# Two fused transformer blocks on one core: one-stage routing with a split router, the output matrix by row halves, linear heads normed beside the product

## The chip, the cores and the metric

One NeuronCore of a Trainium2 chip runs the whole program. The metric is the device time of one execution in microseconds (us), the median of several runs. The engines are PE (TensorE, matmuls), DVE (VectorE), ACT (ScalarE), POOL (GpSimd) and SP (SyncE, which issues the transfers). Tensors are fp32; the big products are made in three fp32r passes of a high and a low part.

## The reference

256 tokens of width 1024 pass a first block (attention, spatial gating, cross attention, 16 routed experts) and a second of two layers. What the change touches:

```python
def hierarchical_moe(h, w_rg, b_rg, w_re, b_re, w_gate, w_up, w_down):   # block 1, h = rms_norm(x, g_moe)
    glog = (t @ w_rg + b_rg); gprob = softmax(glog); gval, gidx = top_k(gprob, 1)
    elog = (t @ w_re + b_re).reshape(-1, N_GROUPS, EXPERTS_PER_GROUP)
    evals, eidx = top_k(elog of group gidx, TOP_K); ew = softmax(evals) * gval
    for e in range(N_EXPERTS): y += combine[:, e:e+1] * ((silu(t @ w_gate[e]) * (t @ w_up[e])) @ w_down[e])

for i in range(DEPTH_2):                                                 # block 2
    u = rms_norm_2(h, norm_attn[i]) @ w_in[i]
    o_a = nsa_attention(...)                                             # mix columns 0..255
    o_b = diff_attention(...)       # rms_norm_2(o, sub_gain) * (1 - lam_init)     256..511
    o_c = gla_mixer(...)            # rms_norm_2(o, norm_gain) * silu(og)          512..767
    o_d = hgrn2_mixer(...)          # rms_norm_2(o, norm_gain) * silu(og)          768..1023
    h = h + concatenate([o_a, o_b, o_c, o_d]) @ w_out[i]
    c = rms_norm_2(h, norm_ffn[i])
    h = h + (swiglu(c) if i % 2 == 0 else moe_swiglu(c, router, ...))    # layer 1: top 2 of 8 experts
    h = h + (p[i] @ ple_w_proj[i]) * sigmoid(rms_norm_2(h, ple_norm[i]) @ ple_w_gate[i])
```

## The kernel before, in words

All weights stream through a ring of 12 raw pieces of 512 KB. SP loads them in the fixed order in which `stream_matrix` and `Experts` add them; ACT makes the high part of a piece (`make_hi`, line 403), DVE the low part (`make_lo`, line 408), both into rings of four; PE multiplies three times (lines 424 to 426) and counts the piece as used. The next two pieces of a product are split ahead, as "early" ones.

The program is a sequence of stages. In a stage every engine runs its own instructions, ordered by semaphores; a stage ends when all engines are through. Each stage is written out by hand, and nothing reorders it.

The first routing is `clear_routing` (the gain row's load, zeroing), `normed_T` (ACT squares and root, line 528 on; DVE scales x; then the stage of `transposes`, lines 480, 518, 502), `route` (the router in full fp32, line 1585, the logits turned, then about thirty tiny DVE steps that pick experts, lines 1618 to 1644 and 2980 to 2993), `place_tokens` (PE counts, DVE writes positions, the dispatch table `disp`, line 2552, and the return table `ret`, line 2555) and `first_gather` (PE gathers tokens for the first four experts bank by bank, line 1286, and DVE and ACT copy banks in turn, line 1297). The second one, in layer 1, is alike without the stacked tables.

The mixers of a layer (`hybrid_mixers`) project, attend (`attend`), add the two halves of each differential head (line 2139), prepare gates, and run the linear pipeline for GLA and HGRN2: PE makes exponents (2316 to 2318) and products (2350), ACT exponentials (2392), DVE decays (2430) and masks (2441), and ACT writes heads into `mix` (2396). Behind it stand `group_norms` for three kinds of heads, a stage that multiplies with the gates (2480), `transposes` of all of `mix` (line 480), and `product` with `w_out`, column chunk by column chunk, each over all rows of the matrix, which adds into x (line 624). Beside this product p is turned.

## Time and profile before

| what | us |
|---|---|
| median of 3 runs (lowest, highest) | 2504.54 (2499.8, 2505.14) |
| the profiled execution, device time | 2508.09 |
| its span in the profile | 2506.3 |
| PE busy | 2270.1 (91%) |
| DVE busy | 1867.1 (74%) |
| ACT busy | 1528.3 (61%) |
| POOL busy | 50.5 (2%) |

Busy shares are averages over stages of very different kind: the two routed expert stages and the dense one fill most of the span, and the routings and mixers are short stages between them. For a change in a short stage one reads that stage's timeline: which engine works, and which waits for it.

### The profile page before, as it was taken

The page shows a single profiled execution, that of the slowest core. Times are in us where ns is not written, and L with a number is a line of the kernel's source. Part 1 is how long each engine was busy: PE and PEld are TensorE (multiplying, and loading weights), DVE is VectorE, ACT ScalarE, POOL GpSimd, SP SyncE. Part 2 cuts the span into 40 slices and gives each one's busy share as a digit, 9 for nine tenths or more (in the row PEclk, how much of TensorE's full clock was granted, in tenths as well). Part 3 has the DMA queues.
Part 4 walks back from the last instruction along what each step waited for, and adds up shares of the span by engine and source line. Part 5 has one row for each costly group of instructions (what it writes and reads, how often), then busy time and mean ns, then how long its engine had stood idle before and what let it go on. Part 6 is the DMA issues. An engine that isn't in the chain of part 4 may idle for free. (4 is left out here: it accounts for less than half of the span.)

```text
span 2506.3 us, 36936 instructions
## 1 busy us (share of the span) xinstructions
PE 2270.1 (91%) x11988; PEld 1858.2 (74%) x11988; DVE 1867.1 (74%) x2075; ACT 1528.3 (61%) x1997; POOL 50.5 (2%) x61
## 2 busy tenths in 40 slices
PE   7988589998987699988986689999999999999997
PEld 6777467776765599976765478888888888888885
DVE  4655588886755645545766569999999999999995
ACT  4554288886532344435532358787878787878784
POOL 0000000000001100000003000000000000000000
PEclk9989799999987899998987789999999999999998
DMA  8433099996630066644620079999999999999991
GB/s 297 134 128 107 9 373 361 353 342 239 188 101 1 22 219 185 186 148 143 179 67 2 30 251 376 336 372 336 377 334 371 336 375 335 374 335 374 336 375 67
DMA packets 280552, 593.81 MB, mean 237 GB/s; under 512 B 26208, under 2 KB 39424, under 8 KB 280320
## 3 DMA queue, kind: packets, MB, share of 16 engines
q1 hardware_dynamic: 280448, 592.45, 66.6%
q8 instruction: 62, 1.02, 0.2%
q14 instruction: 42, 0.34, 0.0%
HBM read 591.32 MB, written 1.05 MB: 236 GB/s over the span
## 5 line engine op out<-in xcount | busy, mean ns | idle before, releaser
L408 DVE TENSOR_TENSOR ring_lo<-ring,ring_hi 128x1024 fp32r<-128x1024 f32 (+1 forms) x1120 | 1337.9, 1215 | 306.8 <-ACT ring_hi L403 249.7
L403 ACT ACTIVATE ring_hi<-ring 128x1024 fp32r<-128x1024 f32 (+1 forms) x1120 | 1162.2, 1053 | 486.0 <-PE psum L426 432.7
L424 PE MATMUL psum<-ring_hi,xg_hi 128*128 128x512 f32 x896 | 356.2, 398 | 5.9 <-PEq L189 3.5
L426 PE MATMUL psum<-ring_hi,xg_lo 128*128 128x512 f32 x896 | 351.0, 392 | 0.0
L425 PE MATMUL psum<-ring_lo,xg_hi 128*128 128x512 f32 x896 | 350.3, 391 | 0.0
L424 PE MATMUL psum<-ring_hi,xT_hi 128*128 128x512 f32 (+2 forms) x512 | 201.5, 394 | 19.2 <-DVE ring_lo L408 10.3
L424 PEld LDWEIGHTS psum<-ring_hi,xg_hi 128*128 128x128 f32 x896 | 169.4, 189 | 40.0 <-issue 3.7
L426 PE MATMUL psum<-ring_hi,xT_lo 128*128 128x512 f32 (+2 forms) x512 | 197.8, 386 | 0.0
L425 PE MATMUL psum<-ring_lo,xT_hi 128*128 128x512 f32 (+2 forms) x512 | 197.7, 386 | 0.0
L426 PEld LDWEIGHTS psum<-ring_hi,xg_lo 128*128 128x128 f32 x896 | 169.1, 189 | 36.3
L425 PEld LDWEIGHTS psum<-ring_lo,xg_hi 128*128 128x128 f32 x896 | 169.6, 189 | 33.9
L424 PE MATMUL psum<-ring_hi,hT_hi 128*128 128x512 f32 x448 | 176.3, 394 | 8.8 <-DVE x L1210 5.2
L425 PE MATMUL psum<-ring_lo,hT_hi 128*128 128x512 f32 x448 | 175.1, 391 | 0.0
L426 PE MATMUL psum<-ring_hi,hT_lo 128*128 128x512 f32 x448 | 175.1, 391 | 0.0
L424 PE MATMUL psum<-xT_hi,ring_hi 128*128 128x256 f32 x480 | 137.2, 286 | 3.2 <-PEq L189 3.2
L425 PE MATMUL psum<-xT_lo,ring_hi 128*128 128x256 f32 x480 | 137.0, 285 | 0.0
L426 PE MATMUL psum<-xT_hi,ring_lo 128*128 128x256 f32 x480 | 136.9, 285 | 0.0
L424 PEld LDWEIGHTS psum<-ring_hi,xT_hi 128*128 128x128 f32 x512 | 98.8, 193 | 40.7 <-DVE ring_lo L408 9.4
L1327 PE MATMUL psum<-ring_hi,xg 128*128 128x512 f32 x256 | 108.8, 425 | 5.8 <-DVE ring_lo L408 3.8
L426 PEld LDWEIGHTS psum<-ring_hi,xT_lo 128*128 128x128 f32 x512 | 98.6, 192 | 19.6
L425 PEld LDWEIGHTS psum<-ring_lo,xT_hi 128*128 128x128 f32 x512 | 99.1, 194 | 18.3
L424 PEld LDWEIGHTS psum<-ring_hi,hT_hi 128*128 128x128 f32 x448 | 84.6, 189 | 29.5 <-issue 12.4
(501 smaller groups left out, 3242.8 us busy)
## 6 DMA issues: line engine op xcount, KB each, us to landing
ring<-in_moe_w_gate_dram SPq DMA_DIRECT2D x224, 512.0 KB, 5.3
ring<-in_moe_w_up_dram SPq DMA_DIRECT2D x224, 512.0 KB, 5.5
ring<-in_moe_w_down_dram SPq DMA_DIRECT2D x224, 512.0 KB, 4.9
ring<-in_w_in_dram SPq DMA_DIRECT2D x76, 512.0 KB, 5.1
ring<-in_w_gate_dram SPq DMA_DIRECT2D x64, 512.0 KB, 5.0
ring<-in_w_up_dram SPq DMA_DIRECT2D x64, 512.0 KB, 5.6
ring<-in_w_down_dram SPq DMA_DIRECT2D x64, 512.0 KB, 5.4
ring<-in_ffn_w_gate_dram SPq DMA_DIRECT2D x28, 512.0 KB, 3.7
```

The lines of the kernel that those rows point to most:

```text
L403: sc.activation(raw_view(ring_hi, FINE, num, a, width), raw_view(ring, RAW, num, a, width), ACT.Copy) \
L408: v.tensor_tensor(raw_view(ring_lo, FINE, num, a, width), raw_view(ring, RAW, num, a, width), raw_view(ring_hi, FINE, num, a, width).bitca ...
L424: pe.matmul(out_, lhsT[0], rhs[0], start=start, stop=False)
L425: pe.matmul(out_, lhsT[0], rhs[1], start=False, stop=False)
L426: return pe.matmul(out_, lhsT[1], rhs[0], start=False, stop=stop)
L1327: pe.matmul(to, lhsT, w[0], start=start, stop=False)
```

## The change

It computes the same. Four things are done.

Routing in one stage. `route` turns x as it is, while ACT squares it; the gain is multiplied into the router's columns, the logits are scaled by 1/rms afterwards. Router and x are split into high and low parts, and 32 fp32r matmuls take the place of 16 in full fp32. Tokens are scaled by one DVE instruction per half. The low parts of the tokens are made in `place_tokens`, the return table in `first_gather`, where ACT makes all copies. As the turned tokens are no longer normed, the branch that runs all tokens through all experts (not taken with these inputs) turns them itself.

Output matrix by row halves. `w_out` streams its upper four row pieces for both column chunks, then the lower ones.

Softmax heads early. The NSA and differential heads (the upper rows' inputs) are normed and turned at the start of the linear pipeline's stage. The add of the differential pairs is a step of `attend`.

Linear heads beside the product. Its first four pieces need only the softmax heads; meanwhile ACT and DVE norm and gate the linear ones, whose norm gain is a column now, applied when the turned heads are copied. Several tiles (`sq_wide`, `kv_twice`, `qkT`) lie in parts of `mix` and `u` that are free at the time.

```diff
+    def stream_matrix_by_halves(w):
+        for half in range(2):
+            for c in range(0, D, FF):
+                for q in range(2 * half, 2 * half + 2):
+                    ws.add(w[q * 2 * P:(q + 1) * 2 * P, c:c + FF].rearrange("(a p) n -> p a n", p=P), 2, FF)
...
+                        if "pairs_to" in j:
+                            both = j["dst"].rearrange("p (n c) d -> p n c d", c=2)
+                            step(v.tensor_tensor(j["pairs_to"], both[:, :, 0, :], both[:, :, 1, :], ALU.add))
...
-                        for k in range(0, KT, 2):
-                            e.wait_ge(g.sem, g.at(k + 1))
-                            l.inc(copy_gathered(v.tensor_copy, k, 0, bank(k)))
...
+                        for half in range(HALVES):
+                            for c in range(2):
+                                l.inc(v.tensor_tensor(ret[:, half, :, c * SLOTS:(c + 1) * SLOTS], disp[:, half, :, :].bitcast(F32),
+                                                      last_bc(comb[:, half, 1:E + 1], SLOTS), ALU.mult))
...
-                        for k in range(1, KT, 2):
+                        for k in range(KT):
...
+    def routed_experts(xn, stacked=None, meanwhile=lambda step: None, placed=lambda: None):
+        place_tokens(N_EXP2 if routed[0] else N_EXP1, stacked, meanwhile)
+        placed()
...
+    def route(gain, row, w, n, xn, finish):
         done, summed, copied = S("router_ready"), S("router_summed"), S("router_copied")
+        turned_x, x_hi, x_lo, w_scaled, w_hi, w_lo = (S(n) for n in ("transposed", "hi_ready", "lo_copied", "squares_scaled", "gates_ready",
+                                                                     "gates_plus_one"))
+        sq, act, rms_done, dve = S("squares_summed"), S("act_chain"), S("rms_done"), S("dve_chain")
...
+                    for b in range(4):
+                        for m in range(4):
+                            k, h = 2 * b + m // 2, m % 2
+                            last = pe.transpose(bank(where[b])[:, m * P:(m + 1) * P], x[:, h, k * P:(k + 1) * P], ident)
+                        turned_x.inc(last)
+                    e.wait_ge(w_lo.sem, w_lo.at(1))
                     for k in range(KT):
-                        for m, part in enumerate(xT):
-                            last = pe.matmul(bank(2)[0:n, 0:SEQ], w[:, k, :], part[:, k, :].bitcast(F32),
-                                             start=(k == 0 and m == 0), stop=(k == KT - 1 and m == 1))
+                        if k % 2 == 0:
+                            e.wait_ge(x_lo.sem, x_lo.at(k // 2 + 1))
+                        for i, w_ in enumerate(w_split):
+                            for j, x_ in enumerate(xT):
+                                last = pe.matmul(bank(2)[0:n, 0:SEQ], w_[:, k, :], x_[:, k, :], start=(k == 0 and i == 0 and j == 0),
+                                                 stop=(k == KT - 1 and i == 1 and j == 1))
...
+                def scalar_first(e):
+                    e.wait_ge(w_scaled.sem, w_scaled.at(1))
+                    w_hi.inc(sc.copy(w_split[0][:], w[:]))
+                    for b in range(4):
+                        e.wait_ge(turned_x.sem, turned_x.at(b + 1))
+                        x_hi.inc(sc.copy(pair_of(xT[0], b), bank(where[b])))
+                    use_table(LOG_EXP)
+                    for h in range(HALVES):
+                        sq.inc(sc.activation(junk[:, h, :], x[:, h, :], ACT.Square, accum_out=ss[:, h:h + 1]))
+                    e.wait_ge(sq.sem, sq.at(HALVES))
+                    act.inc(sc.activation(rms[:], ss[:], ACT.Ln, scale=1.0 / D, bias=eps))
+                    e.wait_ge(act.sem, act.total)
+                    rms_done.inc(sc.activation(rinv[:], rms[:], ACT.Exp, scale=-0.5))
...
+                def vector_first(e, ready):
+                    w_scaled.inc(v.tensor_tensor(w[:], w[:], last_bc(gain[:], n), ALU.mult))
+                    for t in (comb, chosen, place):
+                        dve.inc(v.memset(t[:], 0.0))
+                    dve.inc(v.memset(bank(3, 2), 0.0))
+                    e.wait_ge(w_hi.sem, w_hi.at(1))
+                    w_lo.inc(v.tensor_tensor(w_split[1][:], w[:], w_split[0][:].bitcast(F32), ALU.subtract))
+                    for b in range(4):
+                        e.wait_ge(x_hi.sem, x_hi.at(b + 1))
+                        x_lo.inc(v.tensor_tensor(pair_of(xT[1], b), bank(where[b]), pair_of(xT[0], b).bitcast(F32), ALU.subtract))
+                    e.wait_ge(rms_done.sem, rms_done.at(1))
+                    e.wait_ge(gain_loaded.sem, gain_loaded.total)
+                    for h in range(HALVES):
+                        ready.inc(v.scalar_tensor_tensor(out=xn[:, h, :], in0=x[:, h, :], scalar=rinv[:, h:h + 1], in1=gain_row[:],
+                                                         op0=ALU.mult, op1=ALU.mult))
+                    e.wait_ge(done.sem, done.at(1))
...
-        gla_gain = par("gla_gain", [P, HD], A["gla_norm_2"][layer].partition_broadcast(P))
-        hg_gain = par("hgrn_gain", [P, HD], A["hgrn_norm_2"][layer].partition_broadcast(P))
+        gain_cols = tmp(L2, "linear_gains", [P, 2])
+        for n, name in enumerate(("gla_norm_2", "hgrn_norm_2")):
+            for half in range(2):
+                loads.append((gain_cols[half * HD:(half + 1) * HD, n:n + 1], A[name][layer].rearrange("(d one) -> d one", one=1)))
...
+                          pairs_to=od[:, h, n0 // 2:n0 // 2 + 2, :],
...
+                        else:
+                            e.wait_ge(y_lo.sem, y_lo.at(m + 1))
...
+                    for b in range(2):
+                        if b:
+                            e.wait_ge(od_normed.sem, od_normed.at(1))
+                        for m in range(4):
+                            k, h = 2 * b + m // 2, m % 2
+                            last = pe.transpose(bank(6 + b)[:, m * P:(m + 1) * P], mix[:, h, k * P:(k + 1) * P], ident)
+                        turned_y.inc(last)
...
+                    for b in range(2):
+                        e.wait_ge(turned_y.sem, turned_y.at(b + 1))
+                        y_hi.inc(sc.copy(pair_of(xT[0], b), bank(6 + b)))
...
+                    step(v.tensor_scalar(d_norm[:], d_norm[:], 1.0 - lam_init, None, ALU.mult))
+                    e.wait_ge(od_squared.sem, od_squared.at(1))
+                    step(v.tensor_reduce(od_ss, od_sq, AXX, ALU.add), od_summed)
+                    e.wait_ge(od_root.sem, od_root.at(1))
+                    step(v.tensor_tensor(od, od, last_bc(od_rt, HD), ALU.mult))
+                    step(v.tensor_tensor(od, od, row_bc(d_norm[:], [HALVES, MH]), ALU.mult), od_normed)
...
+                    for b in range(2):
+                        e.wait_ge(y_hi.sem, y_hi.at(b + 1))
+                        y_lo.inc(v.tensor_tensor(pair_of(xT[1], b), bank(6 + b), pair_of(xT[0], b).bitcast(F32), ALU.subtract))
...
+            order = [(c, 2 * half + q) for half in range(2) for c in range(2) for q in range(2)]
...
+                    for i, (p, (c, q)) in enumerate(zip(got, order)):
+                        if i == 4:
+                            e.wait_ge(y_lo.sem, y_lo.at(2))
+                        e.wait_ge(lo_ready, p.n + 1)
+                        w = [raw_view(r, FINE, (p.n, 0), 2, FF) for r in (ring_hi, ring_lo)]
+                        for a in range(2):
+                            k = 2 * q + a
+                            for h in range(HALVES):
+                                last = three_passes(bank(2 * c + h), [x_[:, k, h * P:(h + 1) * P] for x_ in xT],
+                                                    [w_[:, a, :] for w_ in w], k == 0, k == KT - 1)
+                        last.then_inc(used, 1)
+                        if i == 2:
+                            for b in range(2):
+                                e.wait_ge(normed.sem, normed.at(b + 1))
+                                for m in range(4):
+                                    k, h = 4 + 2 * b + m // 2, m % 2
+                                    last = pe.transpose(bank(4 + b)[:, m * P:(m + 1) * P], mix[:, h, k * P:(k + 1) * P], ident)
+                                turned_y.inc(last)
...
+                    squared.inc(sc.activation(squares[:], both, ACT.Square))
+                    make_his(e, not_early(got[:4]))
+                    e.wait_ge(sums.sem, sums.at(1))
+                    act.inc(sc.activation(rt[:], ss[:], ACT.Ln, scale=1.0 / HD, bias=eps))
+                    e.wait_ge(act.sem, act.total)
+                    roots.inc(sc.activation(rt[:], rt[:], ACT.Exp, scale=-0.5))
+                    use_table(SILU)
+                    for n in ("gog", "rog"):
+                        gates.inc(sc.activation(uc(n), uc(n), ACT.Silu))
+                    for b in range(2):
+                        e.wait_ge(turned_y.sem, turned_y.at(b + 1))
+                        y_hi.inc(sc.activation(pair_of(xT[0], 2 + b), bank(4 + b), ACT.Copy, scale=gain_cols[:, b:b + 1]))
+                    make_his(e, got[4:])
+                    use_table(LOG_EXP)
+                    e.wait_ge(p_turned.sem, p_turned.at(1))
+                    p_hi.inc(sc.copy(flat(pT)[0], bank(6)))
+                    make_his(e, early)
+                @block.vector
+                def _(e):
+                    e.wait_ge(squared.sem, squared.at(1))
+                    sums.inc(v.tensor_reduce(ss[:], squares[:], AXX, ALU.add))
+                    make_los(e, not_early(got[:4]))
+                    e.wait_ge(roots.sem, roots.at(1))
+                    dve.inc(v.tensor_tensor(both, both, last_bc(rt[:], HD), ALU.mult))
+                    e.wait_ge(dve.sem, dve.total)
+                    for b, n in enumerate(("gog", "rog")):
+                        at = slice(512 + b * 256, 768 + b * 256)
+                        e.wait_ge(gates.sem, gates.at(b + 1))
+                        normed.inc(v.tensor_tensor(mix[:, :, at], mix[:, :, at], uc(n), ALU.mult))
+                    for b in range(2):
+                        e.wait_ge(y_hi.sem, y_hi.at(b + 1))
+                        y_lo.inc(v.scalar_tensor_tensor(out=pair_of(xT[1], 2 + b), in0=bank(4 + b), scalar=gain_cols[:, b:b + 1],
+                                                        in1=pair_of(xT[0], 2 + b).bitcast(F32), op0=ALU.mult, op1=ALU.subtract))
+                    make_los(e, got[4:])
...
-                            for c in range(2):
-                                dve.inc(v.tensor_tensor(ret[:, h, :, c * SLOTS:(c + 1) * SLOTS], disp[:, h, :, :].bitcast(F32),
-                                                        last_bc(comb[:, h, 1:n + 1], SLOTS), ALU.mult))
...
+    def low_tokens(step):
+        step(v.tensor_tensor(xn_split[1][:], xn[:], xn_split[0][:].bitcast(F32), ALU.subtract))
+    routed_experts(xn_split, (disp1, ret1), low_tokens, routing.close)
```

How the instructions stand. First DVE from the last product's stage to the first pick of the first routing, before (a branch closes or opens a stage; `xn_rows` are the tokens, `gl` and `el` the logits):

```order
L554 TENSOR_SCALAR xn_rows<-x,rinv 128x1024 x2
L189 UNCONDITIONAL_BRANCH
L491 UNCONDITIONAL_BRANCH
L502 SCALAR_TENSOR_TENSOR xT_lo<-psum,c_g_moe,xT_hi 128x256 x8
L189 UNCONDITIONAL_BRANCH
L2973 UNCONDITIONAL_BRANCH
L1604 TENSOR_TENSOR xn_rows<-xn_rows,gain_row 128x2048
L2978 TENSOR_TENSOR xn_moe_lo<-xn_rows,xn_moe_hi 128x2048
L2980 TENSOR_TENSOR gl<-psum,r_b_rg 128x8
L2981 TENSOR_TENSOR el<-psum,r_b_re 128x32
L1618 TENSOR_REDUCE gbest<-gl 128x2
```

and in the changed kernel the same place, in one stage:

```order
L1686 TENSOR_TENSOR router_lo<-router,router_hi 128x160
L1689 TENSOR_TENSOR xT_lo<-psum,xT_hi 128x512 x4
L1693 SCALAR_TENSOR_TENSOR xn_rows<-x,rinv,gain_row 128x1024 x2
L3162 SCALAR_TENSOR_TENSOR gl<-psum,rinv,r_b_rg 128x4
L3164 SCALAR_TENSOR_TENSOR el<-psum,rinv,r_b_re 128x16
L3162 SCALAR_TENSOR_TENSOR gl<-psum,rinv,r_b_rg 128x4
L3164 SCALAR_TENSOR_TENSOR el<-psum,rinv,r_b_re 128x16
L1713 TENSOR_REDUCE gbest<-gl 128x2
```

Three changes of stage are gone, and a scaling that had waited for a stage of its own stands ahead of the logits, which now need the root.

Then DVE behind the linear pipeline, before: the norms, the gates, the turned heads' low parts and the output product with its pieces (`ring_lo`), four stages.

```order
L701 UNCONDITIONAL_BRANCH
L704 TENSOR_TENSOR sq<-mix 128x512 x3
L707 TENSOR_REDUCE gss<-sq 128x8 x3
L710 TENSOR_TENSOR mix<-mix,grt 128x2x256
L712 TENSOR_TENSOR mix<-mix,diff_norm 128x2x256
L710 TENSOR_TENSOR mix<-mix,grt 128x2x256
L712 TENSOR_TENSOR mix<-mix,gla_gain 128x2x256
L710 TENSOR_TENSOR mix<-mix,grt 128x2x256
L712 TENSOR_TENSOR mix<-mix,hgrn_gain 128x2x256
L189 UNCONDITIONAL_BRANCH
L2477 UNCONDITIONAL_BRANCH
L2480 TENSOR_TENSOR mix<-mix,u_111 128x2x256 x2
```

In the changed kernel the linear heads' work stands between low parts of the product's own pieces (`out_sums`, `out_roots` and `linear_gains` belong to them):

```order
L2661 UNCONDITIONAL_BRANCH
L2664 TENSOR_REDUCE out_sums<-out_squares 128x16
L416 TENSOR_TENSOR ring_lo<-ring,ring_hi 128x1024 x2
L2667 TENSOR_TENSOR mix<-mix,out_roots 128x2x512
L2672 TENSOR_TENSOR mix<-mix,u_116 128x2x256 x2
L2675 SCALAR_TENSOR_TENSOR xT_lo<-psum,linear_gains,xT_hi 128x512 x2
L416 TENSOR_TENSOR ring_lo<-ring,ring_hi 128x1024 x4
L2687 TENSOR_TENSOR x<-x,psum 128x512 x2
```

The heads' scaling now stands behind two pieces' low parts and ahead of four others.

Last PE at the opening of the linear pipeline (`lg` and `u` hold the logs of the gates, QD and KD the decayed queries and keys), before:

```order
L2316 MATMUL psum<-consts,lg 128x512
L2317 MATMUL psum<-consts,lg 128x384
L2318 MATMUL psum<-consts,lg 128x128
L2350 MATMUL psum<-QD,KD 64x64 x24
L2350 MATMUL psum<-qkT 64x64 x4
L2352 MATMUL psum<-QD,KD 128x64 x2
```

and in the changed kernel:

```order
L2418 MATMUL psum<-consts,lg 128x512
L2419 MATMUL psum<-consts,lg 128x384
L2420 MATMUL psum<-consts,lg 128x128
L2481 MATMUL psum<-consts,mix 128x128 x8
L2452 MATMUL psum<-QD,KD 64x64 x24
L2452 MATMUL psum<-u_116 64x64 x4
L2454 MATMUL psum<-QD,KD 128x64 x2
```

Eight transposes of `mix` have come between the second unit's exponents and the first products.

## Rows read from the trace of the kernel before

**Rows 1.** Windows over two stretches of the expert stages (busy us, instructions):

```profile
380.00:580.00 200.00, 200.00 (x909) 145.37 (x908) 174.19 (x180) 167.00 (x224) 0.00 (x0) 1.00 0.96 351
...
1500.00:2400.00 900.00, 894.90 (x4154) 742.94 (x4153) 834.68 (x769) 705.13 (x733) 0.00 (x0) 1.00 0.97 355
```

**Rows 2.** Timeline of DVE, first routing (start, duration, line, operands, idle before):

```profile
266.17 1.29 DVE L624 TENSOR_TENSOR x<-x,psum 128x512 f32<-128x512 f32 x2 [1.88 <-PE psum L426]
...
283.95 2.29 DVE L2978 TENSOR_TENSOR xn_moe_lo<-xn_rows,xn_moe_hi 128x2048 fp32r<-128x2048 f32 x1 [2.04 <-ACT xn_moe_hi L3000]
...
289.66 0.16 DVE L1618 TENSOR_REDUCE gbest<-gl 128x2 f32<-128x8 f32 x1
...
296.43 0.19 DVE L2993 TENSOR_TENSOR chosen<-m,goh 128x32 f32<-128x32 f32 x1
...
305.34 2.36 DVE L2555 TENSOR_TENSOR return_p<-dispatch,comb 128x1024 f32<-128x1024 f32 x2
```

**Rows 3.** Timeline of ACT in the same stretch:

```profile
269.40 1.06 ACT L528 ACTIVATE xn_rows<-x 128x1024 f32<-128x1024 f32 x1 [7.55 <-PEq L189]
...
271.94 0.20 ACT L533 ACTIVATE rinv<-rms 128x2 f32<-128x2 f32 x1
...
313.62 0.59 ACT L1297 CAST xg<-psum 128x512 fp32r<-128x512 f32 x1 [0.37 <-PE psum L1286]
```

**Rows 4.** Timeline of PE, the gather of the first routing:

```profile
312.23 0.40 PE L1286 MATMUL psum<-dispatch,xn_moe_lo 128*128 128x256 f32 x2
312.47 0.40 PE L1286 MATMUL psum<-dispatch,xn_moe_hi 128*128 128x256 f32 x2
```

**Rows 5.** Windows before the first routing, and where the linear pipeline ends:

```profile
253.30:256.80 3.50, 3.43 (x8) 2.78 (x9) 2.31 (x2) 2.00 (x2) 0.00 (x0) 0.52 0.02 5
256.80:266.00 9.20, 9.20 (x41) 7.32 (x39) 3.61 (x5) 2.12 (x2) 0.00 (x0) 1.00 0.00 0
266.00:268.00 2.00, 0.13 (x1) 0.00 (x0) 1.47 (x5) 0.00 (x0) 0.00 (x0) 1.00 0.00 0
824.00:830.00 6.00, 2.63 (x12) 2.30 (x12) 1.50 (x3) 0.99 (x4) 2.18 (x5) 0.74 0.00 0
```

**Rows 6.** Timelines of ACT, PE and DVE, tail of layer 0's mixers:

```profile
828.93 0.27 ACT L2396 COPY mix<-psum 128x128 f32<-128x128 f32 x1 [3.30 <-PE psum L2367]
...
839.55 3.65 PE L480 MATMUL psum<-consts,mix 128*128 128x128 f32 x16 [10.65 <-PEq L189]
...
844.87 0.47 PE L424 MATMUL psum<-ring_hi,xT_hi 128*128 128x512 f32 x1 [1.68 <-PEq L189]
...
867.43 0.69 DVE L624 TENSOR_TENSOR x<-x,psum 128x512 f32<-128x512 f32 x1 [3.06 <-PE psum L426]
```

**Rows 7.** Timeline of DVE, second routing:

```profile
1414.42 1.29 DVE L624 TENSOR_TENSOR x<-x,psum 128x512 f32<-128x512 f32 x2 [3.06 <-PE psum L426]
...
1437.56 0.17 DVE L1618 TENSOR_REDUCE best<-lg 128x2 f32<-128x16 f32 x1
...
1441.58 0.17 DVE L1644 TENSOR_TENSOR comb<-one,one 128x16 f32<-128x16 f32 x1
```

**Rows 8.** Timeline of ACT, the tail's table load:

```profile
833.90 1.28 ACT L201 ACT_TABLE_LOAD   x1
```

**Rows 9.** The page's costliest groups, splitting of weights:

```profile
L408 DVE TENSOR_TENSOR ring_lo<-ring,ring_hi 128x1024 fp32r<-128x1024 f32 (+1 forms) x1120 | 1337.9, 1215 | 306.8 <-ACT ring_hi L403 249.7
L403 ACT ACTIVATE ring_hi<-ring 128x1024 fp32r<-128x1024 f32 (+1 forms) x1120 | 1162.2, 1053 | 486.0 <-PE psum L426 432.7
```

**Rows 10.** Timeline of DVE, start of the linear pipeline:

```profile
794.02 1.23 DVE L2441 TENSOR_TENSOR pairs<-psum,consts 128x1024 f32<-128x1024 f32 x1 [3.06 <-PE psum L2352]
```

**Rows 11.** Timeline of DVE, the pairs stage:

```profile
774.77 0.76 DVE L2139 TENSOR_TENSOR mix<-o 128x256 f32<-128x256 f32 x2 [0.54 <-PEq L189]
```

**Rows 12.** Timelines of DVE and SP, start of layer 0:

```profile
631.48 2.36 DVE L2018 TENSOR_TENSOR mix<-x,g_final 128x1024 f32<-128x1024 f32 x2 [6.72 <-DMA g_final<-in_g_final_dram]
...
620.07 0.43 SPq L460 DMA_DIRECT2D hgrn_gain<-in_hgrn_norm_dram  x1
```

More of the change, by code:

```diff
@@ L1576, in route, with _ @@
         with ExitStack() as st:
             logits_T = tmp(st, "logits_T", [n, SEQ])
+            gain_row = tmp(st, "gain_row", [P, D])
+            junk = tmp(st, "x_squares", [P, HALVES, D])
+            ss, rms, rinv = (tmp(st, name, [P, HALVES]) for name in ("ss", "rms", "rinv"))
+            w_split = tmp_split(st, "router", [P, KT, n])
             with stage() as block:
-                sync_stage(block)
+                @block.sync
+                def _(sp):
+                    gain_loaded.inc(sp.dma_start(gain_row[:], row.partition_broadcast(P)), 16)
+                    issue_loads(sp)
@@ L2502, in build, with place_tokens @@
     largest = ctx.enter_context(nc.sbuf_tensor("largest_count", [P, 1], mybir.dt.int32))
-    def clear_routing(gain_row, src):
-        with stage() as block:
-            @block.sync
-            def _(sp):
-                gain_loaded.inc(sp.dma_start(gain_row[:], src.partition_broadcast(P)), 16)
-                issue_loads(sp)
-            dve = S("dve_chain")
-            @block.vector
-            def _(e):
-                for t in (comb, chosen, place):
-                    last = v.memset(t[:], 0.0)
-                v.memset(bank(3, 2), 0.0)
-                dve.inc(last)
-    def place_tokens(n, stacked):
+    def place_tokens(n, stacked, meanwhile):
         counted, dve = S("tokens_counted"), S("dve_chain")
@@ L3017, in build @@
         pT = tmp_split(ple, "pT", [P, PLE // P, SEQ])
[L3018 to L3039 removed]
+        with ExitStack() as L2:
+            hybrid_mixers(layer, L2, pr, pT)
         moe_x = ExitStack()
         xn = tmp(moe_x, "xn_moe", [P, HALVES, D])
[L3043 to L3046 removed]
         if layer % 2 == 0:
+            normed_T(x, g_ffn2[layer], xT, xn)
             all_tokens_experts(lambda h, ex: const("all_ones")[:, 0:1])
```

276 lines of the change are left out of this document (150 added, 126 removed).

## The prediction, as it was recorded before the result

> **What bounds the kernel now.** I read the windows over the long stretches first. In the first routed experts and in the second the matmul engine is busy for 200.00 of 200 us and 894.90 of 900, at full clock, while the DMA share is 0.96 and 0.97 [rows 1]. Nothing in those stages is edited, so they cost what they cost; what can move is the time ahead of them. The ring of weights is full when they begin, in both kernels with the same pieces, so a stage that ends earlier moves all behind it by the same amount.
>
> So I read the timelines of the short stages next. In them engines take turns. In the first routing the products' last add ends at 267.46 (266.17 + 1.29), the first pick of a maximum stands at 289.66, the last mask at 296.43, and the last of the return tables is written at 307.70 (305.34 + 2.36) [rows 2]. In the mixers' tail ScalarE writes the last linear head at 829.20, TensorE turns `mix` at 839.55, starts the product at 844.87, and VectorE gets the result at 867.43 [rows 6]. The long idle times in brackets there (10.65 before the transposes) say that TensorE waits for stages in which only VectorE and ScalarE work.
>
> **First routing, one stage for four.** Before, 22.2 us lie between 267.46 and 289.66. New, on ScalarE: about 0.7 for the router's high part, four copies of a bank at 0.59 that follow each other at some 0.55 (2.3), then two squares and the root, which took 2.7 before, from 269.40 to 272.14 [rows 3]: rinv at 5.7 after the stage opens. Then VectorE scales x by rinv and the gain row, two instructions of 1024 columns. No such form is in the trace; the nearest row takes 2.29 for 2048 columns of two tensors [rows 2], so 2.3 for both, 8.0. The gain row's transfer is issued at the stage's start and has these 5.7 us. Four small ops on the logits (0.16 to 0.2 each) give 8.7. TensorE is beside it: 16 transposes, then 32 matmuls of 256 columns in place of 16 in full fp32. Matmuls of the new kind and width start 0.24 apart for two (312.23 to 312.47) [rows 4]. 32 x 0.12 = 3.9 from 2.5 on is 6.4, with copy and turning back 7.3: hidden below the 8.0 of VectorE. At half clock the matmuls take 7.7, end at 10.2, and the picks start at 11.4 instead of 8.7. The clock is at 1.00 in the 2 us after the product [rows 5], the transposes now fall into these, so I take mostly full clock. With 0.35 for the stage change the saving is 22.2 - 9.05 = 13.1 at full and 10.4 at half clock; I take **12.0**. The high part of the tokens (one copy of 2048 columns, two times 1.0) now lies beside the last picks, which have 2.1 us left after the exponential; uncovered it would cost 2. The low part (2.29) lies beside the counting matmuls, which VectorE waited for.
>
> **Place and gather.** The return tables leave VectorE's chain: 2 x 2.36 = **4.7** saved [rows 2]. They go to the gather stage, beside TensorE, where VectorE has no copies any more; ScalarE takes all eight, 0.59 each [rows 3]. A bank is four matmuls, so one comes every 0.48 at full and 0.96 at half clock; in a mixture of both the eighth copy ends some 0.3 later than the one that stood at 313.62 (0 to 1.2): **+0.3**.
>
> **Second routing.** Add ends at 1415.71, first pick at 1437.56, end at 1441.75 [rows 7]: 21.85 before, 8.9 or 11.5 new: 12.9 or 10.3, taken as **12.0**. Its placing is not changed.
>
> **The tails, twice.** Before, 38.2 us from 829.20 to 867.43; the product alone is 22.5 of it [rows 6]. New: 0.35 stage change, 22.5 product, 8 transposes in the middle (16 took 3.65 at half clock [rows 6], so 0.9 for 8 at full), and a start at half clock. That start is a row that speaks against the change. The old 16 transposes ran just ahead of the product, and the product then started fast. Where a product starts after idling, 8 matmuls take 3.43 us at 0.52 of the clock, against 41 in 9.20 at 1.00 [rows 5], 1.6 lost; the end of the linear pipeline stands at 0.74 [rows 5]. I take 2.2 (0 to 2.7).
>
> Does the new chain beside it stay hidden? ScalarE: squares 1.05, two high parts 2.0, root 0.5, table 1.28 [rows 8], two SiLU of 512 columns at 0.59 like the copies of that size [rows 3], 1.2: 6.0. VectorE: sums 1.2 (half of the 2.29 for 2048 columns), two low parts, then one scaling of 1024 columns and two gatings of 512, about 7.4. A high part costs 1.053 and a low part 1.215 by the page's groups [rows 9]. TensorE comes to its transposes after three pieces of 2.8, at 8.4 at the earliest and 9.9 with the slow start, so the cover is 1 to 2.5 us. Next late is the fifth piece: its high part can only follow the two copies of turned heads, low part ready near 14, TensorE there at 13.7: 0.3. Sum: 0.35 + 22.5 + 0.9 + 2.2 + 0.3 = 26.3, saving **11.9 per layer**, 23.8 (9.0 to 13.5 each).
>
> **What the linear pipeline pays.** Eight transposes stand between the second exponents and the first products; VectorE there waited 3.06 for TensorE [rows 10], so it is the path: 0.9 at full, 1.8 at half clock. The two low copies of VectorE wait for ScalarE's high ones and stand ahead of its first masking, and end about then. I take 1.5 (0.9 to 2.5), **+3.0** for two layers. The squares, sums and scalings of the differential heads lie in the first 4 us, in which VectorE waits for the first exponential; uncovered they would cost 2.5.
>
> **Small stages.** The stage that adds pairs (0.76, 0.54 idle ahead of it, about 775.9 at the next one's start [rows 11]) becomes one add of 128 columns behind the last output: **1.0 per layer** saved, 2.0.
>
> **Transfers.** Two broadcasts go, four columns of 64 words come: two more issues, 0.43 each on SP and a little between [rows 12], ahead of g_final, for which VectorE waits 6.72 until 631.48 [rows 12], with the second chunk's low parts queued behind it and TensorE behind those: **+0.95** in layer 0 (0 to 2). In layer 1 nobody waits for parameters so early.
>
> **Sum**: -12.0 - 4.7 + 0.3 - 12.0 - 23.8 + 3.0 - 2.0 + 0.95 = **-50.2 us**. The profiled execution took 2508.09 (span 2506.3 and 1.8 around it) and would take 2457.9. It is 3.6 above the median of the runs, 2504.54, from which I forecast **2454.3**. The ends of the terms together: 58 saved (13.1, 4.7, 12.9, 27, 2.4, less 1.8) gives 2446; 36 saved (10.4, 4.7 less 1.2, 10.3, 18, 1.4, less 5 and 2) gives 2468.
>
> **Rivals.** (a) The product keeps the half clock. Its transposes and waits break it up; 96 matmuls at 0.43 instead of 0.23 cost 19.5 per layer, 17.3 more than taken, so 2454.3 + 34.6 = 2489. Against it: after 3.43 us at 0.52 the product ahead of the first routing ran at 1.00 to its end [rows 5]. The Trainium skill, TensorE: Matmul & The Clock Gate, section HAM oscillation, warns of this: waits between groups of matmuls can drop the array to half rate each time. (b) The experts give the gain back: with DMA at 0.96 [rows 1], a start that is earlier for TensorE might meet transfers that are not. Then all ahead of the two routed stages but the 11.4 of layer 0's mixers is lost: 2493. Against it: transfers start with the stage, not by the clock on the wall. (c) The other side: the untaken branch of both expert stages grows by the code for turning tokens. If steps of the taken one got longer through instruction loading, 16 and 56 steps share it: 50.2 / 72 = 0.70 us a step is where it decides, and 1 us gives 2526. Against it: TensorE has no gap in 200 us of such steps [rows 1]. (d) The stages are merged but waits stay: heads turned late in the tails and half clock in both routers, 20 to 36 saved, 2468 to 2484.
>
> **Chances.** Forecast 0.76 (2446 to 2468), better than all ends 0.05, (d) 0.10, (a) 0.03, (b) 0.02, (c) 0.02, and 0.02 for anything that ends within 0.2% (5 us), which is about what a measurement tells from no change. Nearly all cases are faster: 0.96, same 0.02, slower 0.02. For 8 in 10 the range takes the forecast's and a little of its neighbours': 2444 to 2471.
>
> **What would show it.** Right: 8 to 10 us from the last add to the first pick in both routings; 26 us from the last linear head to the product's end; TensorE idle under 1 us inside that product; masking in the pipeline 1 to 2 us later after its stage opens; expert steps as long as before. Wrong: a granted clock near 0.5 through the product, TensorE waiting for `mix` or for the fifth piece's low part by more than 2 us, VectorE waiting for the gain row, or expert steps longer than before.

## The result and the profile after

The changed kernel took 2446.36 us, the median of 4 runs (2444.55 to 2454.46), where the kernel before took 2504.84 in the same session (4 runs, 2499.8 to 2507.61). The ratio is 0.977 with a 95% interval of 0.9751 to 0.9789: 58 us saved, where I had forecast 50.2. The profiled execution took 2447.15, its span is 2445.4. One later execution, of the run with the row of the final gain first, took 3279.52 us at a mean granted clock of 0.642, and its ratio leaves it out.

The page of the profile after begins so (the row PEclk is the granted clock in tenths over 40 slices):

```profile
span 2445.4 us, 36780 instructions
...
PE 2250.2 (92%) x11988; PEld 1849.2 (76%) x11988; DVE 1854.6 (76%) x2058; ACT 1529.0 (63%) x1995; POOL 50.4 (2%) x61
...
PEclk9989899999987899999977899999999999999998
```

First the experts, by windows of the kernel after (all engines, then PE's clock, DMA share, GB/s):

```profile
360.00:560.00 200.00, 200.00 (x909) 145.36 (x908) 174.24 (x179) 167.01 (x224) 0.00 (x0) 1.00 0.96 352
...
1440.00:2340.00 900.00, 894.89 (x4155) 742.89 (x4154) 835.12 (x768) 705.18 (x732) 0.00 (x0) 1.00 0.97 355
```

They answer to [rows 1] and are the same: 909 matmuls in 200 us as before. What was won ahead of these stages is kept behind them.

The first routing, in VectorE's timeline of the kernel after:

```profile
264.23 1.28 DVE L632 TENSOR_TENSOR x<-x,psum 128x512 f32<-128x512 f32 x2 [1.88 <-PE psum L434]
...
267.54 2.47 DVE L1689 TENSOR_TENSOR xT_lo<-psum,xT_hi 128x512 fp32r<-128x512 f32 x4
271.23 2.48 DVE L1693 SCALAR_TENSOR_TENSOR xn_rows<-x,rinv,gain_row 128x1024 f32<-128x1024 f32 x2 [1.21 <-ACT rinv L1676]
...
274.29 0.16 DVE L1713 TENSOR_REDUCE gbest<-gl 128x2 f32<-128x8 f32 x1
...
281.83 2.29 DVE L3195 TENSOR_TENSOR xn_moe_lo<-xn_rows,xn_moe_hi 128x2048 fp32r<-128x2048 f32 x1 [0.54 <-PEq L189]
...
285.29 2.49 DVE L2741 TENSOR_TENSOR dispatch<-consts,place 128x1024 fp32r<-128x1024 f32 x2
288.30 4.63 DVE L1328 TENSOR_TENSOR return_p<-dispatch,comb 128x1024 f32<-128x1024 f32 x4 [0.53 <-PEq L189]
```

From the last add's end (265.51) to the first pick are 8.78 us, where [rows 2] have 22.20. The return tables (4.63 for four) begin only when the dispatch tables are done and lie beside the gather. ScalarE and TensorE in that stage:

```profile
270.99 0.20 ACT L1676 ACTIVATE rinv<-rms 128x2 f32<-128x2 f32 x1
272.23 0.36 ACT L1678 COPY logits_T<-psum 20x256 f32<-20x256 f32 x1 [1.04 <-PE psum L1656]
```

```profile
268.37 0.28 PE L1656 MATMUL psum<-xT_hi,router_hi 128*20 128x256 f32 x1 [0.60 <-DVE xT_lo L1689]
...
271.92 0.28 PE L1656 MATMUL psum<-xT_lo,router_lo 128*20 128x256 f32 x1
```

The 32 split matmuls run from 268.37 to 272.2, and the granted clock is 1.00 from 266 to 275. VectorE's scaling of the tokens ends at 273.71, so TensorE is hidden, as supposed.

The tail of layer 0, timelines of ScalarE, TensorE and VectorE of the kernel after:

```profile
806.60 0.27 ACT L2507 COPY mix<-psum 128x128 f32<-128x128 f32 x1 [2.84 <-PE psum L2471]
```

```profile
807.17 0.76 PE L432 MATMUL psum<-ring_hi,xT_hi 128*128 128x512 f32 x1 [0.61 <-PEq L189]
...
811.10 0.40 PE L432 MATMUL psum<-ring_hi,xT_hi 128*128 128x512 f32 x1
...
817.24 1.03 PE L2632 MATMUL psum<-consts,mix 128*128 128x128 f32 x8
...
821.49 0.47 PE L432 MATMUL psum<-ring_hi,xT_hi 128*128 128x512 f32 x1 [0.49 <-DVE ring_lo L416]
```

```profile
812.90 1.29 DVE L2672 TENSOR_TENSOR mix<-mix,u 128x512 f32<-128x512 f32 x2
...
833.18 1.29 DVE L2687 TENSOR_TENSOR x<-x,psum 128x512 f32<-128x512 f32 x2 [1.54 <-PE psum L434]
```

The last head stands at 806.87 and the last add starts at 833.18: 26.31 us, where [rows 6] have 38.23. The transposes at 817.24 have no wait in brackets: the gated heads were done at 814.19. The product starts at half clock: 9 matmuls take the 3.93 us to 811.10, 0.44 each, and then they follow each other by 0.23. In the kernel before, the product started at full clock, and its first matmuls (844.87 on) are 0.23 apart.

Stage by stage, in us, from the two profiled executions:

| stretch | before | after | saved | forecast |
|---|---|---|---|---|
| routing 1, last add to first pick | 22.20 | 8.78 | 13.4 | 12.0 |
| first pick to the experts' first product | 25.90 | 21.82 | 4.1 | 4.4 |
| routing 2, last add to first pick | 21.85 | 8.50 | 13.35 | 12.0 |
| tail, layer 0 and layer 1 | 38.23, 38.23 | 26.31, 27.06 | 11.9, 11.2 | 11.9, 11.9 |
| linear pipeline to last head, both | 45.31, 40.86 | 45.00, 42.41 | 0.3, -1.55 | -1.5, -1.5 |
| last softmax output's start to the next stage, both | 2.15, 2.15 | 1.64, 1.30 | 0.5, 0.85 | 1.0, 1.0 |
| mixers' start to g_final, layer 0 | 14.58 | 14.10 | 0.5 | -0.95 |

The rows sum to 54.5. The spans differ by 60.9; the other 6 us lie in stretches where nothing was edited, 2.0 of them ahead of 266 us. The experiments had to say what these are.

### The profile page after: what moved, and what is told of

It is laid out like the page before. It is cut to its first block and busy times, and to the rows that moved or that the text cites. A ratio compares the mean times of both kernels' runs of the same rounds, so it can differ in the third digit from the quotient of the medians.

```text
span 2445.4 us, 36780 instructions
## 1 busy us (share of the span) xinstructions
PE 2250.2 (92%) x11988; PEld 1849.2 (76%) x11988; DVE 1854.6 (76%) x2058; ACT 1529.0 (63%) x1995; POOL 50.4 (2%) x61
## 5 line engine op out<-in xcount | busy, mean ns | idle before, releaser
L432 PE MATMUL psum<-ring_hi,xT_hi 128*128 128x512 f32 (+2 forms) x512 | 202.1, 395 | 17.9 <-DVE ring_lo L416 11.2
```

Of the source, the lines that this page charges most:

```text
L432: pe.matmul(out_, lhsT[0], rhs[0], start=start, stop=False)
```

## The experiments

Each is the changed kernel with one edit, unless said otherwise. All were timed against the kernel before on the same chip. The changed kernel itself ran beside its two parts and beside the run in which the product waits; the others are set against it by their ratios to the kernel before.

**The changed kernel again, and its two parts alone.** In the second only the functions of routing, placing and gather are changed, in the third only the mixers with their tail.

> The changed kernel itself, timed in more rounds beside the parts of the change, so that their savings can be added up against its own. The traces show 54.7 us saved in the edited stages (13.4 and 13.35 in the routings, 4.6 in placing, less 0.45 in the gather, 11.9 and 11.2 in the tails, 1.4 in the pairs stages, less 1.2 in the linear pipelines) and some 6 us in stretches where nothing was edited. If those 6 us are chance of one execution, the saving over many runs is nearer 55 (about 2450); if they belong to the change, it stays at 58 or more (2447 or less).

> Only the routing part: one stage for four, split router, return tables beside the gather; mixers as before. By the prediction's terms 12.0 + 4.7 - 0.3 + 12.0 = 28.4 saved; by the stages of the trace after 13.4 + 4.6 - 0.45 + 13.35 = 30.9. If the two parts of the change are independent, this saving and that of the mixers' part add up to the whole. Rival: the routing saves its 31 only where the mixers' part has moved other work, then clearly less than 28.

> Only the mixers' part: matrix by halves, heads turned in the linear pipeline, tail beside the product; routing as before. By the prediction's terms 23.8 - 3.0 + 2.0 - 0.95 = 21.85 saved; by the stages of the trace after 23.1 - 1.2 + 1.4 + 0.5 = 23.8. If the remainder of the whole saving (58.5 less 54.7) comes from the clock that the shorter mixers leave behind them, this one saves 26 to 28; if it is chance, 22 to 24.

Measured: the whole 2448.49 (ratio 0.9767, 0.9745 to 0.979); routing alone 2471.76 (0.9865, 0.9845 to 0.9886), 34 us saved; mixers alone 2476.47 (0.9882, 0.9863 to 0.9901), 30 us saved. Together 63 +- 7 beside 58 +- 6: they add up within what is measured, though each is above what was expected of it: 34 against 28.4 and 30.9, and 30 against 22 to 24 (chance) or 26 to 28 (the clock), so the mixers' run confirms neither. The whole saved 58 us again, against "nearer 55" if the rest were one execution's chance: the 4 us beyond the stages' sum are in the medians of both occasions.

The stages themselves repeat: 8.78 for the first routing in all three executions that have it, 26.31 again for the tail of layer 0, 26.41 with the mixers alone. What does not repeat is the unedited rest. From the tail of layer 0 to the stage ahead of layer 1's linear part are 455.12 us before, 452.69 and 452.70 in the two executions of the changed kernel, 451.13 with the routing alone, 453.34 with the mixers alone. (The pairs stage of layer 1 lies in this stretch and is 0.9 shorter where the mixers are edited; apart from it and the pair adds in `attend` the instructions are the same.) And the start of the program up to the first routing, edited nowhere, took from 261.9 to 269.4 us in the 14 profiled executions of this document.

One place shows where it comes from. Windows of TensorE (busy, count, granted clock, DMA share, GB/s) around the same wait of 3.8 us, of the kernel before and then of the one after:

```profile
1168.00:1171.00 3.00, 0.14 (x2) 1.00 0.03 11
1171.00:1174.00 3.00, 2.81 (x16) 0.60 0.24 70
1174.00:1177.00 3.00, 1.32 (x3) 0.50 0.28 57
1177.00:1180.00 3.00, 3.00 (x8) 0.50 0.52 142
1180.00:1183.00 3.00, 3.00 (x11) 0.69 0.78 264
```

```profile
1131.00:1134.00 3.00, 0.06 (x1) 1.00 0.31 109
1134.00:1137.00 3.00, 2.12 (x12) 0.72 0.14 40
1137.00:1140.00 3.00, 1.16 (x7) 0.71 0.43 68
1140.00:1143.00 3.00, 3.00 (x13) 1.00 0.33 57
```

Behind this idle time (1167.0 to 1170.9, and 1131.1 to 1134.9) the clock falls to 0.50 in both. Before it stays there to about 1181, some 10 us; after it is back at 1.00 by 1140. From the wait to the end of the next product this makes 2.5 of the 6 us. No instruction there was edited. In the other executions the stretch moves with no edit in it, so one pair of traces can't tell what of this belongs to the change.

**The product waits for all heads.**

```diff
-                        if i == 4:
+                        if i == 0:
+                            for b in range(2):
+                                e.wait_ge(normed.sem, normed.at(b + 1))
...
+                                turned_y.inc(last)
                             e.wait_ge(y_lo.sem, y_lo.at(2))
...
-                        if i == 2:
-                            for b in range(2):
...
```

> As the changed kernel, but the product of the output matrix starts only when all heads are turned and split, in the same one stage. Theory: the overlap is what the tail saves. The normed and gated linear heads stand 8.4 us after the stage opens, then 8 transposes (1 to 2), two high and two low parts (1.3 and 0.7 behind them): the product starts 11 to 12 us later than now, less the 1.3 to 1.9 that its interrupted middle costs: 9 to 10 us a layer dearer, 2465 or so. Rival: merging stages is what saves, the overlap little: less than 4 us a layer, under 2455.

Measured: 2469.38 (0.9845, 0.9819 to 0.987), 21 us above the changed kernel that ran beside it. The product now begins at 818.46, VectorE's last add at 843.53:

```profile
814.92 1.97 PE L2622 MATMUL psum<-consts,mix 128*128 128x128 f32 x8 [7.08 <-DVE mix L2671]
818.46 0.80 PE L432 MATMUL psum<-ring_hi,xT_hi 128*128 128x512 f32 x1 [1.56 <-DVE xT_lo L2674]
```

The tail takes 35.38 and 35.48 us. So of the 11.9 us of layer 0, the overlap gives 9.1, and all else together 2.85 (8.4 and 2.75 in layer 1). This rest is the merged stage and the softmax heads turned early, less the slow start of the product: here its first 12 matmuls run at half clock, to 823.74. The rival (merging is what saves) falls. The two tails make 17.5 of the 21 us; the other 3.5 lie outside them.

**The softmax heads turned in the tail** instead of the pipeline: their 8 transposes, high and low parts stand at the tail's start, with a wait on them ahead of the first piece.

> As the changed kernel, but the softmax heads are turned and split at the start of the tail instead of in the linear pipeline. The pipeline should get back what I charged it with, 1.5 us a layer: 40.9 long in layer 1 again instead of 42.4. The tail gets a chain of 8 transposes at half clock (1.9), a high part (0.6) and two low parts (1.3) ahead of the product, some 4 us. Net 2 to 3 us a layer dearer, 2453 to 2455. Rival: the transposes cost the pipeline nothing that lasts, then 4 us a layer dearer, 2457.

Measured: 2455.81 (0.9799, 0.978 to 0.9818), 0.3% above the changed kernel's ratio, 4 us by the stages of its trace. The tail grew to 29.37 and 29.82 (3.06 and 2.76 more, where I expected some 4). The pipelines took 42.17 and 43.86 where the changed kernel has 45.00 and 42.41: one 2.8 shorter, one 1.5 longer. So my 1.5 a layer can't be read from the whole length. Unedited, the pipeline of layer 0 took 45.31 and 43.41 in two executions, with the edit 43.06 to 45.13 in seven; the clock moves it more than the transposes do. It can be read at the first masking in layer 1, where the clock is alike: it starts 8.54 and 8.55 us after the pipeline without the transposes in it, 9.63 or 9.64 in six executions with them, and 8.65 here. They cost 1.1.

**The router unsplit**, 16 matmuls of hi and lo tokens by the whole matrix in full fp32.

```diff
-                        for i, w_ in enumerate(w_split):
-                            for j, x_ in enumerate(xT):
-                                last = pe.matmul(..., w_[:, k, :], x_[:, k, :], ...)
+                        for j, x_ in enumerate(xT):
+                            last = pe.matmul(..., w[:, k, :], x_[:, k, :].bitcast(F32), ...)
```

> As the changed kernel, but the router's matrix is not split: each of the 16 products of tokens and router runs in full fp32, in the same one stage (the router's split is still made and not used). In the trace after, the 32 short matmuls end at 272.2 and VectorE's scaling of the tokens at 273.6, so the matmuls are hidden by 0.4. Unsplit they took 8.7 us before at a changing clock, 6.9 at full: from 268.4 they end at 275.3, the picks start 2.5 to 3 us later in each routing, 5 to 6 us dearer in all (2453 or so). Rival: the split buys nothing since VectorE is the bound there, then 2448, no dearer.

Measured: 2456.35 (0.981, 0.9793 to 0.9827). VectorE of this run:

```profile
267.93 2.48 DVE L1692 SCALAR_TENSOR_TENSOR xn_rows<-x,rinv,gain_row 128x1024 f32<-128x1024 f32 x2 [1.20 <-ACT rinv L1675]
272.93 0.22 DVE L3161 SCALAR_TENSOR_TENSOR gl<-psum,rinv,r_b_rg 128x4 f32<-128x4 f32 x1 [2.52 <-PE psum L1660]
...
273.60 0.16 DVE L1712 TENSOR_REDUCE gbest<-gl 128x2 f32<-128x8 f32 x1
```

The wait of 2.52 us on TensorE stands where none was. From the last add to the picks are 11.39 us, 2.61 more, and 2.35 more in the second routing, 5.0 in both as expected; the ratios differ by more, 0.4% or 10 us, and the other 5 are not explained. The split is needed for the saving to be whole.

**The return tables back** among the dispatch tables, the gather's copies on VectorE and ScalarE in turn.

> As the changed kernel, but the return tables are written between the dispatch tables again, and the gather's copies go to VectorE and ScalarE in turn. The tables cost 2 x 2.36 on VectorE's chain; the copies in turn give back the 0.45 that ScalarE alone takes longer. 4.2 us dearer: dispatch to the experts' first product in the trace 7.9 instead of 3.2 us after the last table, about 2452. Rival: nothing, if the gather's end is set by TensorE and the clock: then no dearer than 1 us.

Measured: 2454.0 (0.9805, 0.978 to 0.9831). From the first pick to the experts' first product: 25.82 us instead of 21.82. The tables cost 4.0, net of the gather's copies: nearly the whole of 4.1. By the ratios this run is 9 us dearer; the other 5 are not explained.

**The row of the final gain first**, with a semaphore of its own.

```diff
+                        if with_final:
+                            gain_loaded.inc(sp.dma_start(g_row[:], ...), 16)
                         for dst, src in loads:
                             params_loaded.inc(sp.dma_start(dst, src), 16)
```

> As the changed kernel, but in the mixers' first stage of layer 0 the row of the final gain is fetched first and has a semaphore of its own, where before VectorE waited for all 14 small transfers, the last of them this one (issued 6.4 us after the first, landed 7.7 after its issue, waited for 6.25 us). If the place in the queue is what it waits for, it lands 6 us earlier, ScalarE's root (606.3) becomes the last, and TensorE's gap of 3.55 us before the second chunk closes: 3 to 5 us saved, 2444. Rival: the row waits for transfers of weights that were issued before all of them, lands hardly earlier, and nothing is saved.

Measured: 2446.19 (0.9767, 0.9752 to 0.9782), no difference in the median. The issues of this row, of the changed kernel and of this one (KB, us to landing):

```profile
g_final<-in_g_final_dram SPq DMA_DIRECT2D x1, 512.0 KB, 7.7
```

```profile
g_final<-in_g_final_dram SPq DMA_DIRECT2D x1, 512.0 KB, 5.6
```

The row is used 7.77 us after the stage's start instead of 14.10, and VectorE, which waited 6.25 us in the changed kernel (first row), no longer waits for it:

```profile
611.34 2.36 DVE L2118 TENSOR_TENSOR mix<-x,g_final 128x1024 f32<-128x1024 f32 x2 [6.25 <-DMA g_final<-in_g_final_dram]
```

```profile
605.17 2.36 DVE L416 TENSOR_TENSOR ring_lo<-ring,ring_hi 128x1024 fp32r<-128x1024 f32 x2
607.45 2.35 DVE L2124 TENSOR_TENSOR mix<-x,g_final 128x1024 f32<-128x1024 f32 x2
```

TensorE's gap of 3.6 us before the second chunk is gone, and the linear part begins 3.4 us earlier, counted from the mixers' start. The expected 2444 was not seen.

**Waits of the pipeline filled.** Transposes of a constant that nobody reads, 12 ahead of the first and of the third crossing, 8 ahead of the last output.

```diff
                     def crossing(n):
+                        if n == 1:
+                            e.wait_ge(y_lo.sem, y_lo.at(2))
+                            fill(6, 12)
+                        elif n == 5:
+                            e.wait_ge(taken_o.sem, taken_o.at(5))
+                            fill(6, 12)
```

> As the changed kernel, with 12 transposes of a constant into an unused part of a bank in each of two waits of 1.8 us in the linear pipeline, and 8 in the wait of 1.1 us before its last output; nobody reads them. Theory: the clock falls to half some 4 us after such an idle stretch (1.8 idle at 776 and at 797, 0.50 from 780.7 and from 801), and the slow start of the tail's product, 1.9 us in layer 0 and 2.9 in layer 1, is inherited from that. If filled waits keep the clock, the product starts at 1.00 and the pipelines' ends get faster too: 3 to 8 us saved, 2440 to 2445. Rival: the clock falls all the same, and the fillers cost 0 to 3 us.

Measured: 2456.15 (0.9802, 0.9786 to 0.9819), slower than the changed kernel, with pipelines of 49.49 and 47.71 us. The second filling waited for a copy (first row below, TensorE), and the clock, 1.00 until then, fell behind that wait (windows of TensorE):

```profile
803.39 2.82 PE L2425 MATMUL psum<-consts 128*128 128x128 f32 x12 [3.67 <-ACT mix L2520]
```

```profile
776.00:800.00 24.00, 23.02 (x496) 1.00 0.01 3
800.00:802.00 2.00, 0.00 (x0) 1.00 0.00 0
803.00:819.00 16.00, 15.00 (x111) 0.50 0.06 17
```

So the wait was moved to an earlier copy (`taken_o.at(4)`, `fill(7, 12)`), and then both edits were joined:

> As the run with filled waits, but the second filling goes to the bank whose output was copied 4 us before, so that it waits for nothing; in that run it waited 3.67 us for ScalarE's copy, and the clock fell there, while behind the first filling it stayed at 1.00 from 776 to 802, where the changed kernel fell to 0.50 at 780.7. Theory: now the clock stays at 1.00 to the end of the pipeline and into the tail, pipeline 42 instead of 45 us in layer 0, tail's product 1.9 and 2.9 us faster: 4 to 8 us saved against the changed kernel, 2440 to 2444. Rival: idling for other reasons (the stage change, the last output's wait) brings the clock down all the same: pipelines about as long as now, tails 26.3 and 27.1, and 0 to 2 us dearer.

> Both: waits filled as in the run beside this one, and the row of the final gain first in the queue (3.2 us saved by the stages of its trace, not seen in the median). The candidate for a version better than both kernels: 2437 to 2442 if the filling works, 2445 to 2448 if not.

> The version with both (waits filled, row of the final gain first) once more on another occasion, since its lead over the changed kernel (2442.7 against 2446.4 and 2448.5, ratios 0.9748 and 0.9767) is smaller than the two intervals. If the lead is real, the ratio is 0.973 to 0.976 again; if it was chance, 0.976 to 0.979.

Measured: filled alone 2445.53 (0.976, 0.9739 to 0.9781). Both edits 2442.74 (0.9748, 0.9726 to 0.977), and again 2439.78 (0.9744, 0.9727 to 0.9762). The same stretch at the kernel after and then with filled waits (windows of TensorE):

```profile
776.00:780.00 4.00, 2.26 (x69) 1.00 0.00 0
781.00:783.00 2.00, 2.00 (x4) 0.50 0.03 8
784.00:800.00 16.00, 13.85 (x338) 1.00 0.01 2
801.00:811.00 10.00, 8.20 (x28) 0.50 0.10 27
```

```profile
772.00:780.00 8.00, 7.61 (x159) 1.00 0.01 2
781.00:783.00 2.00, 2.00 (x10) 1.00 0.03 8
784.00:800.00 16.00, 14.90 (x338) 1.00 0.01 2
801.00:811.00 10.00, 7.96 (x47) 1.00 0.12 34
```

The clock stays at 1.00 from 772 into the product. The tails take 24.48 and 24.51 us instead of 26.31 and 27.06, so the slow start cost 1.8 and 2.6. The pipelines take 42.89 and 41.10 instead of 45.00 and 42.41. Of these 7.8 us the trace loses 4.7 again in the stretch between the layers (457.42 long here), and the median, expected at 2440 to 2444, shows little.

The two effects don't hold alike. At the end of the pipeline they do: in both layers of all three runs with this filling the product starts at 1.00 and the tail takes 24.48 to 24.53 us, and in every other run with edited mixers the product starts at 0.50. In the middle they don't. The run with both edits fell there in spite of the filling (windows of TensorE, layer 0):

```profile
776.00:780.00 4.00, 3.41 (x71) 1.00 0.00 0
781.00:783.00 2.00, 2.00 (x4) 0.50 0.00 0
801.00:811.00 10.00, 7.98 (x50) 1.00 0.09 28
```

Its pipelines took 44.18 and 44.17, those of its repetition 44.17 and 41.09. And in layer 1 of the changed kernel the same wait, unfilled, was followed by no fall:

```profile
1312.80 1.05 PE L2428 MATMUL psum<-QD,KD 32*128 32x128 f32 x8 [1.82 <-DVE KD L2549]
```

```profile
1313.00:1317.00 4.00, 3.93 (x75) 1.00 0.02 4
1317.50:1319.50 2.00, 2.00 (x73) 1.00 0.00 0
```

So the wait alone does not decide whether the clock falls in the middle, and what does stays open.

With both edits the kernel is 0.2 to 0.25% ahead of the changed one by the ratios, on both occasions. The intervals overlap that of the changed kernel, which did not run beside them, so this lead is likely, not certain.

## Why the prediction was right

The likeliest case came true, 8 us beyond its centre and just inside the range of 2446 to 2468. The terms alone don't bring it there: by the stages it would be 2450, and some 4 us that no term holds came on top. That the time is 0.4 us inside the edge and not outside is luck. Point by point:

- **First and second routing** (12.0 each): 13.4 measured in both. The chain is as I wrote it (scaling of the tokens last, TensorE hidden); I had set 13.1 for full clock against 10.4 for half, and taken something between. The clock was at 1.00. Here the term was mis-sized by 1.4, twice. The unsplit router (2.6 and 2.35 us dearer) shows that TensorE's hiding was no matter of course: only 0.7 us lie between the logits' turning (272.65, 0.30 long) and VectorE's first use of them at 273.62.
- **Place and gather** (4.7 less 0.3): 4.1. The tables alone are 4.0 by the run that puts them back.
- **Tails** (11.9 each): 11.9 and 11.2. Of the pieces, the transposes hold the product up from 817.24 to 818.03, 0.79 (0.9), the fifth piece's stall 0.49 (0.3), the slow start 1.8 and 2.6 (2.2, by the filled runs), the cover was 3 us (1 to 2.5). In layer 1 half clock lasts from 1341.35 to 1346.99, 13 matmuls instead of 9: that is its missing 0.7. The prediction did not separate what the overlap gives, 9.1, from the rest.
- **Linear pipeline** (+1.5 each): +1.55 in layer 1 and nothing in layer 0 in the two traces. In layer 0 this is inside what the clock does to that stage, 43 to 45 us with the same instructions. In layer 1 the seven executions with the edited pipeline, unfilled, took 42.34 to 43.16 us, the two without the edit 40.86 and 40.88. The first masking is 1.1 us late (1 to 2 was the sign); that the rest of the 1.5 is the transposes' too is not shown.
- **Pairs stage** (1.0 each): 0.5 and 0.9.
- **Two more issues ahead of the final gain** (+0.95): the issues do take longer, 6.4 us from first to last instead of 4.7, but the row landed 7.7 us after its issue instead of 9.9, and VectorE waited 6.25 instead of 6.72. This step failed in its sign: I took the landing to follow the issue by a fixed time. It holds in the other executions: 9.9 and 10.0 us where the mixers are unedited, 5.9 to 7.7 where they are edited and the row is last. Why it lands sooner stays open.
- **The sum.** 54.5 by stages against 50.2. The other 4 us (58.5 by medians) or 6 (60.9 by spans, with a profiled execution of before that is 3.3 above its median) lie outside the edited stages. One place of them is shown above, a fall of the clock that lasted 10 us before and some 3.4 after. Why it lasted longer in the one stays open, and so does whether all of the rest is of this kind.

Rival (a), half clock through the product: 0.50 for 3.9 and 5.6 us at the product's start, then 1.00 to its end in both layers, with the transposes and the 0.49 of waiting inside it. What the Trainium skill, TensorE: Matmul & The Clock Gate, section HAM oscillation, warns of, half rate behind waits between groups of matmuls, did happen beside it, in the pipeline: a wait of 1.8 us at 776 and at 797, and 0.50 from 781 and again from 801. With filled waits the second fall was gone in all six pipelines, the first in three of them only. Inside the product half clock would have cost 17 us a layer. The trace does not show it there, but no wait in the product was longer than 0.49 us, so the warning was not put to the test. Rivals (b) and (c): the routed stages took 297.89 instead of 297.77 and, from their first product to the end, 1046.00 instead of 1047.02; neither gave anything back. (The 11.4 that rival (b) keeps for layer 0's mixers leaves out the prediction's own +0.95; with it the rival's time is 2494.) Rival (d), waits that stay: no wait over 0.5 us in the product, full clock in both routers.

## What to carry to other kernels

Where engines take turns in short stages around a long product, ask which half of the product's input is ready early, and order the weights so that this half comes first: 9 us a layer here, three times what the merged stage and the softmax heads turned early gave together. Check with the trace that what is laid beside the new chain really ends before it; a router left in full fp32 would have given back 2.5 of the 13.4 us each time. And sum by stages: the new routings repeat to 0.02 us between executions and the overlapped tails to 0.7, but the pipelines differ by 2 us, the stretch between the layers by 5 and the start by 7.5 with the same instructions. So one execution's span can't price an edit of that size, and even medians of single edits stood 3 to 5 us beyond their stages here.

## What the runs showed of the hardware

I had not expected how much TensorE's clock moves these stages. Behind waits of 1.8 and 3.8 us it fell to 0.50, some 4 to 5 us after the engine had gone idle, when it was busy again; it stayed there 3 us (780.7 to 783.7, and 1135.3 to 1138.7) or 10 (801 to 811, and 1171.6 to 1181.8 in the kernel before). It did not fall each time: in layer 1 it stayed at 1.00 behind 1.82 us, and with a filled wait (0.52 us left) it fell at 781 in one execution. Transposes of a constant in the waits near the end of the pipeline (12, 1.48 us at full clock, and 8) kept it at 1.00 into the product in six pipelines of six. In the run whose filling had waited 3.67 us, the 16 us behind it ran at 0.50. And a transfer's landing doesn't follow its issue by a fixed time: the same row took 9.9 us, 7.7, or 5.6 when it was issued first. Its place in the queue is not all of it, since issued last it also took 5.9 us in one execution.
